# First projection: second chunk loaded and split in pieces, one weight piece with its own signals, third load ahead of six small ones

## The reference, cut to what matters

```python
def rms_norm(x, g):
    xf = x.astype(jnp.float32)
    y = xf * lax.rsqrt(jnp.mean(xf * xf, axis=-1, keepdims=True) + NORM_EPS)
    return (y * g.astype(jnp.float32)).astype(x.dtype)
...
    proj = xn @ w_in
    q_a, kv_a, k_rope, conv_in = jnp.split(proj, [o1, o2, o3], axis=-1)
```

## Time and profile before

| what | value |
|---|---|
| device time, median of 3 runs (lowest, highest) | 1077.48 us (1076.65, 1077.51) |
| the profiled execution's own time | 1078.06 us |
| its span in the profile | 1076.3 us |
| granted TensorE clock, mean over the span | 0.998 |
| PE busy | 1063.3 us (99%) |
| DVE, ACT, POOL busy | 775.4, 611.6, 348.3 us |
| moved by DMA | 182.10 MB, mean 169 GB/s |

### The profile page before, as it was taken

The page is one execution under the profiler, slowest core; times in us unless marked ns, Lnnn a source line. Parts: engine busy times, 40 slices in busy tenths (PEclk is TensorE's granted clock), DMA queues, the critical chain, the costliest instruction groups (busy, mean ns, idle before and its releaser), DMA issues.

```text
span 1076.3 us, 21627 instructions
## 1 busy us (share of the span) xinstructions
PE 1063.3 (99%) x8591; PEld 1029.9 (96%) x8591; DVE 775.4 (72%) x1392; ACT 611.6 (57%) x1141; POOL 348.3 (32%) x393
## 2 busy tenths in 40 slices
PE   9999999999999999999999999999999999999997
PEld 8978999999999999999999999999999999999886
DVE  5877689887678788768887545794466567887355
ACT  5658565556546667866665443663336546665431
POOL 0105334334302421455665111200034334665000
PEclk9999999999999999999999999999999999999999
DMA  8562647775655534145555554654405567555552
GB/s 248 134 195 80 197 123 212 205 205 170 204 175 178 180 114 154 44 140 174 178 176 162 191 192 162 220 195 161 154 31 176 187 194 235 171 184 192 191 190 93
DMA packets 196327, 182.10 MB, mean 169 GB/s; under 512 B 7136, under 2 KB 185731, under 8 KB 196099
## 3 DMA queue, kind: packets, MB, share of 16 engines
q1 hardware_dynamic: 195091, 175.67, 52.4%
q0 software_dynamic: 976, 4.99, 1.3%
q10 hardware_dynamic: 160, 0.07, 0.0%
HBM read 177.33 MB, written 1.05 MB: 166 GB/s over the span
## 4 chain that ended last, share of the span: by engine, by line
PE 88%; DVE 4%; ACT 3%; DMA 3%; SPq 1%; issue 1%; POOL 0%; DVEq 0%; ACTq 0%; POOLq 0%
PE ps L2173 24%; PE ps L2174 23%; PE ps L2175 23%; PE ps L2820 3%; PE ps L2819 3%; PE ps L2818 3%; PE ps L2785 1%; PE ps L2370 1%; PE ps L2641 1%; DVE wlo L1485 1%; DMA raw<-w_in 1%; ACT whi L918 1%; PE ps L2763 1%; DMA raw<-ffn_w 1%; PE ps L2405 1%
## 5 line engine op out<-in xcount | busy, mean ns | idle before, releaser
L1485 DVE TENSOR_TENSOR wlo<-raw,whi 128x1024 fp32r<-128x1024 f32 x314 | 392.0, 1286 | 159.6 <-ACT whi L918 158.7
L918 ACT ACTIVATE whi<-raw 128x1024 fp32r<-128x1024 f32 x312 | 314.8, 1053 | 187.4 <-PE ps L2175 128.5
L2173 PE MATMUL ps<-xh,whi 128*128 128x256 f32 (+1 forms) x880 | 247.9, 282 | 2.4 <-DVE wlo L1485 1.3
L2175 PE MATMUL ps<-xh,wlo 128*128 128x256 f32 (+1 forms) x880 | 245.4, 279 | 0.0
L2174 PE MATMUL ps<-xl,whi 128*128 128x256 f32 (+1 forms) x880 | 245.3, 279 | 0.0
L2173 PE MATMUL ps<-xrh,whi 128*128 128x274 f32 (+2 forms) x832 | 240.5, 289 | 0.7 <-DVE wlo L1485 0.7
L2175 PE MATMUL ps<-xrh,wlo 128*128 128x274 f32 (+2 forms) x832 | 237.6, 286 | 0.0
L2174 PE MATMUL ps<-xrl,whi 128*128 128x274 f32 (+2 forms) x832 | 237.6, 286 | 0.0
L2173 PEld LDWEIGHTS ps<-xh,whi 128*128 128x128 f32 x880 | 165.4, 188 | 3.7 <-issue 1.2
L2174 PEld LDWEIGHTS ps<-xl,whi 128*128 128x128 f32 x880 | 165.4, 188 | 0.1
L2175 PEld LDWEIGHTS ps<-xh,wlo 128*128 128x128 f32 x880 | 165.3, 188 | 0.0
(11 more groups left out here) (406 smaller groups left out, 2088.3 us busy)
## 6 DMA issues: line engine op xcount, KB each, us to landing
raw<-ffn_w SPq DMA_DIRECT2D x128, 512.0 KB, 4.6
raw<-ret_w_in SPq DMA_DIRECT2D x48, 512.0 KB, 4.5
raw<-even_w_in SPq DMA_DIRECT2D x24, 512.0 KB, 4.8
raw<-w_ffn_gate SPq DMA_DIRECT2D x22, 512.0 KB, 4.0
raw<-w_ffn_up SPq DMA_DIRECT2D x22, 512.0 KB, 5.3
raw<-w_ffn_down SPq DMA_DIRECT2D x16, 512.0 KB, 4.1
raw<-ret_w_out SPq DMA_DIRECT2D x16, 512.0 KB, 4.1
raw<-w_in SPq DMA_DIRECT2D x10, 512.0 KB, 5.4
```

Source lines behind the costliest of these rows:

```text
L918: A(w_half(whi, 2 * use + slot, s), raw_half(raw, 2 * use + slot, s), ACT.Copy).then_inc(w_hi_ready, 1)
L1485: V.tensor_tensor(w_half(wlo, c, s), raw_half(raw, c, s), f32(w_half(whi, c, s)), ALU.subtract).then_inc(w_lo_ready, 1)
L2173: T.matmul(dst, w[0], x[0], start=first, stop=False)
L2175: return T.matmul(dst, w[1], x[0], start=False, stop=last)
```

## The change

Waits, signals and the order of the queue change; the arithmetic does not.

- The loads of row tiles 4 and 5 of chunk 0 signal on `third_in`; row tiles 6 and 7 are loaded by one transfer each.
- Chunk 1 is loaded in three transfers (row tiles 0 to 3 on `next_in`, 4 and 5, 6 and 7), and its first half is split in two quarters on ACT and DVE instead of as one half. PE starts chunk 1 when the low part of its first quarter is there.
- The third quarter of chunk 0 signals `third_lo`, and PE waits for that instead of for x tile 5.
- The six small loads (taps, meta tokens, lambdas) move from ahead of chunk 2's load to behind it.
- Two pairs of semaphores are merged into one each (`p_split`, `gate_split`), with the same instructions waiting at the same places.

```diff
-                    sp.dma_start(d[:, 4:6], s[:, 4:6]).then_inc(raw_landed[0], 16)
-                    sp.dma_start(d[:, 6:8], s[:, 6:8]).then_inc(raw_landed[0], 16)
+                    sp.dma_start(d[:, 4:6], s[:, 4:6]).then_inc(third_in, 16)
+                    for k in (6, 7):
+                        sp.dma_start(d[:, k:k + 1], s[:, k:k + 1]).then_inc(raw_landed[0], 16)
+                elif j == 1:
+                    d, s = view(1, KD, 256), rows(w_in, KD)[:, :, 256:512]
+                    sp.dma_start(d[:, 0:4], s[:, 0:4]).then_inc(next_in, 16)
+                    for k in (4, 6):
+                        sp.dma_start(d[:, k:k + 2], s[:, k:k + 2]).then_inc(raw_landed[1], 16)
                 else:
-                    columns(c, c % 2, w_in, KD, 256 * j, 256 if j < 2 else o3 - 512)
+                    columns(c, c % 2, w_in, KD, 512, o3 - 512)
+                    load_meta()
...
-            act.wait_ge(raw_landed[0], 32)
+            act.wait_ge(third_in, 16)
             first_high(2).then_inc(first_hi, 1)
             x_high(6)
+            act.wait_ge(raw_landed[0], 32)
             first_high(3).then_inc(w_hi_ready, 1)
             x_high(7)
-            split_at(1)
+            act.wait_ge(next_in, 16)
+            second_high(0).then_inc(first_hi, 1)
+            second_high(1).then_inc(w_hi_ready, 1)
+            act.wait_ge(raw_landed[1], 32)
+            A(w_half(whi, 1, 1), raw_half(raw, 1, 1), ACT.Copy).then_inc(w_hi_ready, 1)
...
-            first_low(2)
+            first_low(2).then_inc(third_lo, 1)
...
             x_lows((7,))
-            split_at(1)
+            dve.wait_ge(first_hi, 3)
+            second_low(0).then_inc(third_lo, 1)
+            dve.wait_ge(w_hi_ready, 3)
+            second_low(1).then_inc(w_lo_ready, 1)
+            split_at(1, (1,))
...
-                    pe.wait_ge(x_ready, X_A + (6 if k == 4 else k + 1))
+                    wait(pe, third_lo, 1 if k == 4 else 0)
+                    pe.wait_ge(x_ready, X_A + k + 1)
...
-                    product(c, c % 2, outs, rows_x1, TOK1, 256, kt=6, order=range(6), last=False)
+                    pe.wait_ge(third_lo, 2)
+                    for k in range(2):
+                        for dst, col, m in outs:
+                            three(dst, tile(c, 256 * k + col, m), [v[:, k, TOK1] for v in rows_x1], k == 0, False)
+                    product(c, c % 2, outs, rows_x1, TOK1, 256, kt=4, order=range(2, 6), first=False, last=False)
```

More of the change, by code:

```diff
@@ L399, in x_turned, with w_quarter, raw_quarter @@
             return ps[4 + k // 2][:, N1 * (k % 2):N1 * (k % 2) + N1]
[L401 to L407, removed]
+        def w_quarter(w, c, q):
+            return w[:, c, :].rearrange("p (a n) -> p a n", a=2)[:, :, 256 * q:256 * q + 256]
+        def raw_quarter(c, q):
+            return raw[:, c, 512 * q:512 * q + 512].rearrange("p (a n) -> p a n", a=2)
         x_rms, squares_diag = ps[0][:, N1:2 * N1], sq[:, :, 0:P]
@@ L562, in deep, with load_meta @@
                 repeat(sp, 2, turn)
+            def load_meta():
+                sp.wait_ge(set_up, 8)
+                for j in range(TG):
+                    taps = a["conv_w"][0][j:TAPS:TG, :].rearrange("i (g c) -> i g c", c=32)
+                    sp.dma_start(cw_rows[0:taps.shape[0], :, j, :], taps).then_inc(small_in, 16)
+                sp.dma_start(meta_rows[:], a["meta_tokens_2"]).then_inc(small_in, 16)
+                sp.dma_start(lam_rows[:], a["diff_lambda_2"].rearrange("a b c -> a (b c)")).then_inc(small_in, 16)
             w_in = a["w_in"][0]
@@ L585, in _ @@
                             sp.dma_start(to[starts_at[name]:starts_at[name] + n, :], src).then_inc(small_in, 16)
[L586 to L591, removed]
             sp.dma_start(pt, a["p"][0, 0].rearrange("(t p) n -> p t n", p=P)).then_inc(pos_in, 16)
@@ L999, in first_high, with second_high @@
             def first_high(q):
-                return A(first_quarter(whi, q), raw_quarter(q), ACT.Copy)
+                return A(w_quarter(whi, 0, q), raw_quarter(0, q), ACT.Copy)
+            def second_high(q):
+                return A(w_quarter(whi, 1, q), raw_quarter(1, q), ACT.Copy)
             def x_high(k):
@@ L1063, in _ @@
             act.wait_ge(pt_done, 1)
-            A(ph[:, :, :], ps[5][:, :].rearrange("p (k n) -> p k n", k=2), ACT.Copy).then_inc(p_hi, 1)
+            A(ph[:, :, :], ps[5][:, :].rearrange("p (k n) -> p k n", k=2), ACT.Copy).then_inc(p_split, 1)
             for j in range(4):
@@ L1211, in _ @@
                     act.wait_ge(gate_in, 16 * 2 * KD)
-                    A(gw_hi[:, :], gw_raw[:, :], ACT.Copy).then_inc(gate_hi, 1)
+                    A(gw_hi[:, :], gw_raw[:, :], ACT.Copy).then_inc(gate_split, 1)
                 if j == 2:
@@ L1826, in finish_e @@
                 if j == 1:
[L1827 to L1828 removed]
+                    dve.wait_ge(gate_split, 1)
+                    V.tensor_tensor(gw_lo[:, :], gw_raw[:, :], f32(gw_hi)[:, :], ALU.subtract).then_inc(gate_split, 1)
                 if j >= 2:
```

20 lines of the change are left out of this document (10 added, 10 removed).

## The result

| | before | after |
|---|---|---|
| device time, median of 22 runs each (us) | 1077.22 | 1078.35 |
| lowest, highest | 1075.99, 1078.40 | 1077.41, 1082.61 |
| profiled execution, its span | 1078.06, 1076.3 | 1078.14, 1076.3 |

The ratio is 1.0013, with a 95% interval of 1.0007 to 1.0019. The forecast was 0.9 us faster; the kernel is 1.1 us slower. By the prediction's bound of 0.2% (2.15 us) that is no change, to which it gave a chance of 0.89, but the time is outside the forecast range (1075.6 to 1078.3) by 0.05, the interval excludes a gain, and the mechanism forecast did not deliver. The two profiled executions hide this: they differ by 0.08, because the traced one of before lies 0.84 above its median. So I compare positions inside the traces, not their spans.

The account below looks back on a forecast made before the run. PE is 99% busy, so only its stops can give time; PE gains 1.4 us, but chunk 2's load chain gives 0.94 - 0.05 = 0.9 at 47.87 and limits it. Median 1077.48 - 0.9 = 1076.6, range 1075.6 to 1078.3.

Parts of the forecast that it names:

- Part 1: Chunk 0's third quarter: its own signal removes PE's 0.4 us wait before row tile 4; chunk 0 ends 0.48 earlier.
- Part 2: Chunk 1 in pieces: PE's 0.85 stop and slow first matmul go; with chunk 0's 0.48, PE gains 1.4 us.
- The price of the pieces elsewhere: Chunk 1's split on ACT and DVE: one instruction more each, under 0.1 us, beside slack.
- Part 3, issue: SP's queue: chunk 2's load goes at 12.33 instead of 13.27, 0.94 earlier, after DVE's fourth quarter signals at 12.31.
- The landing follows the issue: Chunk 2's load: keeping 4.85 us from issue to landing, it lands at 17.6 instead of 18.56.
- the bound of 7.9: Chunk 2's load: longest landing time after the second issue at 12.8, putting the landing at 20.7.
- B: Chunk 2 not issued earlier or chunk 3 late; PE's gain waited off at 47.87, 0 to 0.5 earlier; chance 0.23.
- C: Six small loads land late, `others` on PE starts 1.9 later, end 1.3 later, 1078.8; chance 0.06.
- D: Each added transfer delays chunk 1's landing by a whole landing, 3.3 us; end 3.6 later, 1081.1; chance 0.02.
- the wait of 1.1 at chunk 6: PE's wait for chunk 6 at 47.87 comes near 47.0 and grows from 0.64 to 1.1, limiting the gain to 0.9.

Follow-up runs that it names:

- before_five: The kernel before with five of the ten matmuls ahead of the first transpose left out; median 1077.21 against 1076.78, ratio 1.0000.
- five_fewer: The changed kernel with five of the ten matmuls ahead of the first transpose left out; median 1077.07 against before's 1077.09, ratio 0.9994.
- both_away: The changed kernel with five matmuls fewer ahead of the first transpose and DVE splitting chunk 1's first half in one instruction; 1076.74 against before's 1077.74, ratio 0.9995.
- early_fill_dve_one: early_fill with DVE splitting the first half of chunk 1 in one instruction; median 1077.64 against before's 1076.94, ratio 1.0000.
- fill: The changed kernel with three unread matmuls between the transposes of taps and of meta tokens; median 1078.28 against before's 1077.40, ratio 1.0005.
- early_fill: fill with chunk 2's two halves also issued among the row loads; median 1077.13 against before's 1077.51, ratio 0.9998.
- meta_last: The changed kernel with the six small loads moved behind `p`, `positions` and the table; median 1078.66 against before's 1077.51, ratio 1.0012.
- whole_early: The changed kernel with chunk 1 loaded and split whole and chunk 2's halves issued among the row loads; 1077.87 against before's 1077.31, ratio 1.0006.
- shift: The changed kernel with twenty 64-column matmuls instead of ten of 128 ahead of the first transpose; median 1081.54 against before's 1077.31, ratio 1.0044.

## Why the prediction was wrong

- **Part 1** was right: the stop before row tile 4 went, a tiny one before row tile 6 came (the matmul at 12.83 takes 0.37), and chunk 0 is 0.40 shorter (forecast 0.48).
- **Part 2** was right in what it promised at its place: the stop of 0.85 went. With part 1 PE's gain is 0.89 on top of a start 0.52 late, 1.41 (forecast 1.4). The late start is no part of the change: chunk 0 begins between 8.12 and 8.78 in most traces. The price of the pieces elsewhere was estimated at nothing ("one instruction more each, under 0.1 us, beside slack"). This term failed: it is 0.63 at 384 us.
- **Part 3, issue**: 12.79 instead of 12.33, since DVE's fourth quarter, for which it waits, moved with the late `x`. That is 0.48 of the 0.94.
- **Part 3, "The landing follows the issue"**: this step failed. I took 4.85 for the transfer because little else in flight had changed; it took 5.83, so the landing came at 19.05 and not at 17.6, and the bound of 7.9 had this case in it. What I did not look at is the queue that no line of the kernel issues. In before the 16-KB packet lay at the load's front edge (tail 0.87), the change put it inside (1.8). The 4.85 itself already had such a packet in it: without one the transfer took 3.5 (before_five) to 4.0 (five_fewer, both_away).
- **The wait that took its place** was not among the rivals. I asked who waits for PE and for the small loads but not when PE's chunk 2 could start at the earliest. DVE scales chunk 0's products behind the split of chunk 2 ("20.25" to "22.21" in the chain), so PE's early arrival met the late landing. The 0.9 that PE had gained became a stop of 0.76 and, through the clock, 1.6 us more, of which 1.03 went into the places of before's waits at 47.87 and near 63.
- **Rivals**: B had the place right (nothing of PE's gain arrives) and the sign wrong. C's late small loads did not happen. D, by which each added transfer would cost a whole landing, is refuted: ACT took chunk 1's second half at 13.12 instead of 12.66, with one transfer more, and not 6 us later. The Trainium skill (DMA: Bandwidth & Descriptors, "Rules for kernel authors") asks to merge many small transfers, and says that under 64 KB one pays mostly overhead. The pieces here are of 128 KB and more, so it does not state what D made of it; the fixed cost of about 2 us of its "Anatomy of one DMA" is given for transfers issued from GpSimd, and these are issued from SP.
- The forecast's number came out once the two side effects were removed: both_away is 0.88 earlier at 64 us, for which 0.9 was forecast, and its median 1076.74 is near 1076.6. Much of that is luck: its start was 1.2 late, chunk 2 landed at 17.24, and the wait of 1.1 at chunk 6, by which the chain was to set the 0.9, did not come at all.

What is shown: the late landing goes with the instruction packet (eight traces with it inside the load, tail 1.57 to 2.14; eight with it at the end or behind, 0.18 to 0.37; the one late signal of sixteen), the 0.6 at 384 is DVE's one instruction. What is open: why the packet costs up to 2 us when it takes 1, why most such packets cost little, and when one comes.

## What to carry to other kernels

Before you cost an edit "at nothing" because its engine has slack, remember that it also shifts that engine's later instructions: here one more on DVE cost 0.6 us 370 us later. When you move a load on the critical path, look in the DMA queues for packets of kind "instruction", see whether one now falls into it, and look at its last landing signal, not at its last data. When PE is made to arrive earlier, work out the earliest time at which its next stage can be released; a stop among small transposes costs more than its length if the clock falls. Where single events of 0.5 us decide, compare the starts of the same matmuls between traces and repeat the trace; spans and medians of few runs mislead.

## What the runs showed of the hardware

- A packet of 16 KB on the instruction queue, 0.9 us long, inside a load of 320 KB: the last 2 to 3% of its packets came 1.6 to 2.1 us behind the rest, one of the transfer's 16 signals 0.9 to 2.7 us behind the others, and the whole transfer took 5.3 to 6.2 us from issue to landing instead of 3.2 to 4.5. Of all weight transfers with such a packet in flight one in four had its last signal more than 0.7 us late, of those without one in 55.
- The clock at chunk 2: it fell to 0.50 in six traces. In five of them PE had stopped for 0.23 to 1.57 us behind the small transposes; in early_fill_dve_one it had not stopped, and its last work had been small transposes and three matmuls of 128 columns. It stayed at 1.00 in fill and early_fill, whose PE did the same work, and in meta_last, where PE stopped for 0.53 and 0.29 around the transposes. In after 17 matmuls took 3.64 us instead of 2.05 by it.
- The clock at the start: the traces have no record of it at first, and the windows view prints 1.00 there. The first record, granted 1.00, starts at 4.2 to 7.1 us in 14 traces, at 8.0 to 10.3 in the three kernels with five matmuls fewer, at 9.91 in whole_early and at 13.69 in shift. Ahead of it eight transposes of `x` took 1.97 us; in after, mostly behind it, 1.20 and 1.09.
- Matmuls of 64 and of 128 columns on full float32, all into one bank, took 0.22 and 0.23 us per record, both ahead of the first clock record. Behind it, in after, four records of 128 columns took 0.61 us; ahead of it, in five_fewer, four took 1.06.
- Chunk 0's first matmul started between 8.12 and 8.78 in those 14 traces, with the second half of `x` landed between 7.22 and 7.89; in whole_early, with `x` at 7.99, at 10.16 by the clock. The start of an execution alone is worth as much as this whole change.
